# A hybrid decoder block on one core: four weight stages stream 512 columns per matmul instead of 256

## The chip, the core and the metric

The kernel runs on one core of a Trainium2 chip. Time is device microseconds of one launch; the median of three runs is given. The engines of the core work side by side: PE (TensorE) multiplies, DVE (VectorE) and ACT (ScalarE) do elementwise work and read the matmul results from the eight PSUM banks (128 partitions x 512 float32 each), POOL (GpSimd) does a little, SP (SyncE) issues the transfers from memory. They are tied together by semaphores that the kernel sets by hand.

## The reference, cut to what matters

One decoder layer on 256 tokens of width 2048, in float32:

```python
y = rmsnorm(x); u = y @ w_in                   # queries, keys, values, gates of three branches
mk, mv = split(rmsnorm(mem) @ w_mem_kv)        # memory keys and MEMORY VALUES, 1024 columns each
a = sparse_attention(...)                      # 8 heads
r = group_norm(retention(q, k, v)) * silu(g)   # g: RETENTION GATE, 1024 columns of u
m = memory_attention(mq, mk, mv)               # 4 heads
s = sum(sigmoid(gate_b) * (branch_b @ w_br_b)) # merged, 256 x 2048
x = x + rmsnorm(s @ w_o)                       # OUTPUT PROJECTION, 2048 x 2048
z = rmsnorm(x) @ w_up                          # 2048 x 11264
z = gelu(conv3(z[:, :5632])) * conv3(z[:, 5632:])
out = x + rmsnorm(z @ w_down)                  # DOWN PROJECTION, 5632 x 2048
```

The four products in capitals are those that the change touches.

## The kernel before, in words

**Three products for one.** Each float32 operand is split into a rounded part (`_hi`) and the remainder (`_lo`), both in the type fp32r. A product is then hi x hi + hi x lo + lo x hi: three matmuls in a row, each with a weight load of its own (PEld in the profile).

**Quads and chunks.** The weights come in quads: 4 chunks of 512 KB, each 4 row tiles (of 128) x 256 columns. Chunk c has slot c of `wraw`, `whi` and `wlo`. For a chunk, SP loads `wraw[c]` (line 255 or 265), ACT makes `whi[c]` (line 461), DVE makes `wlo[c]` (line 679), and PE runs 24 matmuls of 256 columns: 4 row tiles x 2 halves x 3 products. ACT's step for the next quad's chunk c waits until PE has finished chunk c of this quad (`pe_done`), DVE's step waits for ACT's, SP's next load waits for DVE's (`lo_done`). The helper `ahead(q, chunks)` stands for this work on the next quad, and what else ACT and DVE do is written between such calls.

**Two forms.** In `chunk_t` (lines 1064 to 1066) a 128 x 128 piece of the weights is the stationary operand and the 256 tokens stream. In `chunk_n` (lines 1077 to 1079) 128 tokens are stationary and 256 weight columns stream. The four stages of the change use `chunk_n`. Each result of a quad fills one bank: 256 columns for tokens 0 to 127, then 256 for tokens 128 to 255.

**The four stages.** Memory values (`mv`, 4 quads), retention gate (`rg`, 4 quads) and output projection (`wo`, 8 quads) accumulate a quad in bank 0 or 1, in turn. A bank is drained while the next quad runs in the other: `mv` by one DVE copy (line 690), `rg` by ACT's tanh (line 570) and DVE's product (line 866), `wo` by two ACT squares (line 613) and a DVE product (line 953). PE waits for `evac[b]` before it takes bank b again. The down projection runs in 11 steps of 2 quads. Here each chunk is a group of 256 output columns over 512 rows of `w_down`, goes to bank 2 + g % 4, and is added to `M` by DVE (line 1015); `s_dn` counts these adds, and group g waits for the add of group g - 4.

**Loops.** Between two down steps stand 4 quads of the up projection (`chunk_t`). Two steps (1152 matmuls) form the body of one hardware loop of 5 trips at the end of the kernel; the 11th down step follows it. `mv`, `rg` and most of `wo` are hardware loops of 2, 2 and 3 trips with 192 matmuls in a body. After `wo` and after the last down step there is a mean square (DVE lines 703 and 704, POOL line 386) and a normalisation (line 970) before PE or the output can go on. After `rg` the first thing in the retention is `inner` (line 1314), two matmuls into bank 3 behind the first chunk of the next quad.

Of the kernel before, what the change touches and what calls it, by code (L numbers as in the profile page):

```python
# [25 lines left out]
P = 128  # L26
# [32 lines left out]
PHASES = [("mq", 4, 4), ("mk", 4, 4), ("mv", 4, 4), ("nq", 4, 4), ("kv0", 3, 3), ("mix", 7, 3),  # L59
          ("rqk", 4, 4), ("rv", 4, 4), ("rg", 4, 4),  # L60
          ("bg0", 8, 8), ("br0", 4, 8), ("bg1", 8, 8), ("br1", 4, 8), ("bg2", 8, 8), ("br2", 4, 8),
          ("wo", 8, 8), ("up0", 4, 4), ("ffn", 6 * (STEPS - 1), 4 * (STEPS - 1)), ("dn", 2, 0)]
# [63 lines left out]
def build(nc, x, mem, w_in, cmp_pe_k, cmp_w1_k, cmp_w2_k, cmp_pe_v, cmp_w1_v, cmp_w2_v, rel_bias,  # L126
# [3 lines left out]
    with ctx:  # L130
# [71 lines left out]
        s_swap, s_rgt, s_stats = sem("halves_swapped"), sem("ret_gate_tanh"), sem("stats_made")  # L202
# [45 lines left out]
        def _(sp):  # L248
            def quad(q, src):

                for c in range(4):
                    if q:

                        sp.wait_ge(lo_done, 4 * (q - 1) + c + 1)
                    sp.dma_start(wraw[:, c], src(c)).then_inc(loaded[c], 16)  # L255

            def loop(q0, trips, per, sources):

                with sp.Fori(0, trips) as i:
                    free = [sp.snap(4 * per * i + (4 * (q0 - 1) + k + 1)) for k in range(4 * per)]  # L260
                    src = sources(i)
                    for j in range(per):
                        for c in range(4):
                            sp.wait_ge(lo_done, free[4 * j + c])
                            sp.dma_start(wraw[:, c], src[j](c)).then_inc(loaded[c], 16)

            def cols(w, base, count=2):
# [4 lines left out]
                return sources  # L272

# [32 lines left out]
            loop(Q0["mk"], 4, 2, cols(w_mem_kv[:, :, :], 0))  # L306
# [16 lines left out]
            loop(Q0["rg"], 2, 2, cols(w_in, C_RQ + 8 * GW))  # L323
# [15 lines left out]
            for n in range(2):  # L339
                quad(Q0["wo"] + n, lambda c: rows(w_o, 4 * c, GW * n))  # L340
# [3 lines left out]
            loop(Q0["wo"] + 2, 3, 2, cols(w_o, 2 * GW))  # L344
# [18 lines left out]
            loop(Q0["ffn"], STEPS - 1, 6, step)  # L363
            for j in range(2):
                quad(Q0["dn"] + j, down((STEPS - 1) * 512)[j])
# [89 lines left out]
        def _(act):  # L455
# [107 lines left out]
            with act.Fori(0, 2) as i:  # L563
                for j in range(2):
                    q = 2 * i + (Q0["rg"] + j)
# [41 lines left out]
            with act.Fori(0, 4) as i:  # L607
                for j in range(2):
                    q = 2 * i + (Q0["wo"] + j)
                    ahead(q, (0, 1, 2))  # L610
                    act.wait_ge(pe_done, 4 * q + 4)
# [4 lines left out]
                    ahead(q, (3,))  # L616
# [38 lines left out]
            ahead(Q0["dn"], (0,))  # L655
            for g in range(8):
                if g < 3:
                    ahead(Q0["dn"], (g + 1,))
                act.wait_ge(s_dn, 4 + 8 * (STEPS - 1) + g + 1)
                for t in range(TT):  # L660
                    e = nc.scalar.activation(h_hi[:, 2 * g + t, :], M[:, t, GW * g:GW * (g + 1)], ACT.Square,
# [766 lines left out]
```

## Time and profile before

| | |
|---|---|
| median of 3 runs | 1865.62 us (1865.15 to 1865.78) |
| profiled execution: span, first to last instruction | 1862.0 us |
| what lies around it (median less span) | 3.6 us |
| PE busy | 1775.8 us, 95% (14,505 matmuls) |
| DVE busy | 1057.9 us, 57% |
| ACT busy | 789.5 us, 42% |
| DMA | 328.19 MB, 57.6% of the engines' time |

The whole duration of the profiled execution is not listed apart from its span; the 3.6 us are the median less the span. A matmul's row shows its start and its length; because matmuls are pipelined, the distance between the starts of two of them is what one costs, and the length is longer than that. The granted clock of TensorE is 1.0 at 2.4 GHz and 0.5 at 1.2 GHz.

### The profile page before, as it was taken

Reading aid. Unit: us, or ns where it says so; the run is one execution under the profiler, and the core shown is the slowest. Engines: PE = TensorE matmul, PEld = TensorE weight load, DVE = VectorE, ACT = ScalarE, POOL = GpSimd, SP = SyncE. Lnnn points to the kernel's source line nnn. Section 1 sums busy time; section 2 is a strip of 40 time slices with the busy share of each in tenths; the row PEclk is TensorE's granted clock in tenths of the full one; section 3 lists DMA queues with packets and bytes.
Section 4 is the critical chain, followed back from the end, with each engine's and each line's share of the span. In section 5 each row is a group of like instructions: output and inputs, shape, how many; then the busy total and the mean of one; then the engine's idle time right before and its main releaser. Section 6 shows DMA issues by size and latency. Waiting matters only on the chain.

```text
span 1862.0 us, 36931 instructions
## 1 busy us (share of the span) xinstructions
PE 1775.8 (95%) x14505; PEld 1763.1 (95%) x14505; DVE 1057.9 (57%) x1321; ACT 789.5 (42%) x1036; POOL 42.2 (2%) x47
## 2 busy tenths in 40 slices
PE   7599999999999999999999799989999998999997
PEld 6499999899999999999999799989989998998997
DVE  5254557566565444454564566655665664664666
ACT  5233335444433334434444454434444443443443
POOL 0000100000031000000000000000000000000000
PEclk9799999999999999999999899999999999999999
DMA  8655457645555566666575356655555554555553
GB/s 244 140 183 184 138 158 242 188 136 153 174 163 164 184 181 180 196 192 183 174 233 186 124 182 196 188 160 172 184 185 158 184 183 154 182 185 161 181 182 113
DMA packets 321460, 328.19 MB, mean 176 GB/s; under 512 B 12239, under 2 KB 318528, under 8 KB 320832
## 3 DMA queue, kind: packets, MB, share of 16 engines
q1 hardware_dynamic: 321344, 326.45, 57.6%
q8 instruction: 96, 1.57, 0.3%
q14 instruction: 20, 0.16, 0.0%
HBM read 321.69 MB, written 3.67 MB: 175 GB/s over the span
## 4 chain that ended last, share of the span: by engine, by line
PE 51%; issue 42%; DVE 2%; DMA 2%; SPq 1%; ACT 1%; POOL 0%; DVEq 0%; POOLq 0%; ACTq 0%
PE bank L1064 11%; PE bank L1066 11%; PE bank L1065 11%; PE bank L1077 5%; PE bank L1079 5%; PE bank L1078 5%; DMA wraw<-in_w_in 1%; SPq L255 1%; DVE wlo L679 1%; DVE arena L970 0%; ACT whi L461 0%; PE bank L1131 0%; PE bank L1193 0%; PE bank L1295 0%; PE bank L1274 0%
## 5 line engine op out<-in xcount | busy, mean ns | idle before, releaser
L679 DVE TENSOR_TENSOR wlo<-wraw,whi 128x1024 fp32r<-128x1024 f32 x592 | 728.7, 1236 | 655.1 <-ACT whi L461 653.5
L461 ACT ACTIVATE whi<-wraw 128x1024 fp32r<-128x1024 f32 x592 | 625.3, 1059 | 946.7 <-PE bank L1066 649.4
L1064 PE MATMUL bank<-h_hi,whi 128*128 128x256 f32 x2688 | 769.0, 286 | 10.4 <-DVE wlo L679 7.5
L1065 PE MATMUL bank<-h_lo,whi 128*128 128x256 f32 x2688 | 764.6, 284 | 9.6 <-issue 9.6
L1066 PE MATMUL bank<-h_hi,wlo 128*128 128x256 f32 x2688 | 764.5, 284 | 0.0
L1064 PEld LDWEIGHTS bank<-h_hi,whi 128*128 128x128 f32 x2688 | 520.0, 193 | 12.8 <-DVE wlo L679 8.1
L1066 PEld LDWEIGHTS bank<-h_hi,wlo 128*128 128x128 f32 x2688 | 520.0, 193 | 10.0 <-issue 10.0
L1065 PEld LDWEIGHTS bank<-h_lo,whi 128*128 128x128 f32 x2688 | 519.8, 193 | 0.2
L1077 PE MATMUL bank<-whi,r_hi 128*128 128x256 f32 x704 | 199.2, 283 | 0.0
L1078 PE MATMUL bank<-wlo,r_hi 128*128 128x256 f32 x704 | 199.2, 283 | 0.0
L1079 PE MATMUL bank<-whi,r_lo 128*128 128x256 f32 x704 | 199.2, 283 | 0.0
L1077 PEld LDWEIGHTS bank<-whi,r_hi 128*128 128x128 f32 x704 | 135.2, 192 | 0.0
L1078 PEld LDWEIGHTS bank<-wlo,r_hi 128*128 128x128 f32 x704 | 135.2, 192 | 0.0
L1079 PEld LDWEIGHTS bank<-whi,r_lo 128*128 128x128 f32 x704 | 135.2, 192 | 0.0
L1064 PE MATMUL bank<-m_hi,whi 128*128 128x256 f32 x384 | 108.7, 283 | 0.0
L1065 PE MATMUL bank<-m_lo,whi 128*128 128x256 f32 x384 | 108.7, 283 | 0.0
L1066 PE MATMUL bank<-m_hi,wlo 128*128 128x256 f32 x384 | 108.7, 283 | 0.0
L1077 PE MATMUL bank<-whi,m_hi 128*128 128x256 f32 x384 | 108.7, 283 | 0.0
L1078 PE MATMUL bank<-wlo,m_hi 128*128 128x256 f32 x384 | 108.7, 283 | 0.0
L1079 PE MATMUL bank<-whi,m_lo 128*128 128x256 f32 x384 | 108.7, 283 | 0.0
L1077 PE MATMUL bank<-whi,h_hi 128*128 128x256 f32 x320 | 92.4, 289 | 1.1 <-DVE wlo L679 1.1
L1079 PE MATMUL bank<-whi,h_lo 128*128 128x256 f32 x320 | 91.0, 285 | 0.0
(202 smaller groups left out, 1759.2 us busy)
## 6 DMA issues: line engine op xcount, KB each, us to landing
wraw<-in_w_in SPq DMA_DIRECT2D x200, 512.0 KB, 3.7
wraw<-in_w_up SPq DMA_DIRECT2D x176, 512.0 KB, 3.8
wraw<-in_w_down SPq DMA_DIRECT2D x88, 512.0 KB, 3.4
wraw<-in_w_mem_kv SPq DMA_DIRECT2D x32, 512.0 KB, 4.6
wraw<-in_w_o SPq DMA_DIRECT2D x32, 512.0 KB, 3.5
wraw<-in_w_br_mem SPq DMA_DIRECT2D x16, 512.0 KB, 3.4
wraw<-in_w_br_nsa SPq DMA_DIRECT2D x16, 512.0 KB, 4.0
wraw<-in_w_br_ret SPq DMA_DIRECT2D x16, 512.0 KB, 3.3
```

Source lines behind the costliest of these rows:

```text
L255: sp.dma_start(wraw[:, c], src(c)).then_inc(loaded[c], 16)
L461: nc.scalar.activation(whi[:, c], wraw[:, c], ACT.Copy).then_inc(hi_done, 1)
L679: V.tensor_tensor(wlo[:, c], wraw[:, c], whi[:, c].bitcast(F32), ALU.subtract).then_inc(lo_done, 1)
L1064: T.matmul(o, wh, xh, start=first and k == 0 and t == 0, stop=False, skip_group_check=True)
L1065: T.matmul(o, wh, xl, start=False, stop=False, skip_group_check=True)
L1066: e = T.matmul(o, wl, xh, start=False, stop=last and k == CK - 1, skip_group_check=True)
L1077: T.matmul(o, xh, wh, start=first and k == 0 and t == 0, stop=False, skip_group_check=True)
L1078: T.matmul(o, xh, wl, start=False, stop=False, skip_group_check=True)
L1079: e = T.matmul(o, xl, wh, start=False, stop=last and k == CK - 1, skip_group_check=True)
```

## The change

The four stages stream 512 weight columns per matmul. A chunk is still 512 KB, but now 2 row tiles x 512 columns, and has 12 matmuls (2 token halves x 2 row tiles x 3 products). A result of 512 columns fills two banks, one for each half of the tokens. Two quads together (`octet`, 8 chunks) make one 512-column group in banks 0 and 1 or 2 and 3. In the down projection a group of 512 columns has two chunks and the bank pair 2, 3 or 4, 5; group n waits for the adds of group n - 2. The drains become two instructions for each pair. The loops of `mv`, `rg` and `wo` are written out.

```diff
@@ phases: (name, quads, groups that are drained)
-... ("mv", 4, 4) ... ("rg", 4, 4) ... ("wo", 8, 8)
+... ("mv", 4, 2) ... ("rg", 4, 2) ... ("wo", 8, 4)
@@ slot views and loads
+        def wide(buf, c):
+            return buf[:, c].rearrange("p k n -> p (k n)").rearrange("p (k n) -> p k n", k=2)
+            def wide_cols(w, base):
+                def sources(i):
+                    at = sp.snap(2 * GW * i + base)
+                    return [lambda c, j=j: rows(w, 8 * j + 2 * c, at, 2 * GW, 2) for j in range(2)]
+                return sources
-            loop(Q0["mk"], 4, 2, cols(w_mem_kv[:, :, :], 0))
+            loop(Q0["mk"], 2, 2, cols(w_mem_kv[:, :, :], 0))
+            loop(Q0["mv"], 2, 2, wide_cols(w_mem_kv[:, :, :], MH * MD), into_wide)
...
-                return [lambda c, j=j: w[:, :, (4 * j + c) * GW:(4 * j + c + 1) * GW] for j in range(2)]
+                return [lambda c, j=j: w[:, 2 * (c % 2):2 * (c % 2) + 2, (4 * j + 2 * (c // 2)) * GW:(4 * j + 2 * (c // 2) + 2) * GW]
+                        for j in range(2)]
@@ ACT: retention gate and output projection
-                    ahead(q, (0, 1, 2))
-                    act.wait_ge(pe_done, 4 * q + 4)
-                    act.wait_ge(evac[1 - j], i + (G0["rg"] // 2 + j))
-                    nc.scalar.activation(work[:, W_RGT:W_RGT + 512], ps[j][:, :], ACT.Tanh, scale=0.5).then_inc(s_rgt, 1)
-                    ahead(q, (3,))
+                ahead(q)
+                ahead(q + 1, (0, 1, 2))
+                act.wait_ge(pe_done, 4 * (q + 1) + 4)
+                for t in range(TT):
+                    if 2 * i + t:
+                        act.wait_ge(s_rgv, 2 * i + t)
+                    nc.scalar.activation(work[:, W_RGT:W_RGT + 512], ps[2 * i + t][:, :], ACT.Tanh, scale=0.5).then_inc(s_rgt, 1)
+                ahead(q + 1, (3,))
...
-                    for t in range(TT):
-                        e = nc.scalar.activation(work[:, 512 * j + S * t:512 * j + S * (t + 1)], bank(j, t), ACT.Square,
-                                                 accum_out=sq[:, 0, t, bass.ds(2 * i + j, 1)])
-                    e.then_inc(s_sq, 1)
+                for t in range(TT):
+                    nc.scalar.activation(work[:, 512 * t:512 * (t + 1)], ps[2 * (i % 2) + t][:, :], ACT.Square,
+                                         accum_out=sq[:, 0, t, i:i + 1]).then_inc(s_sq, 1)
@@ DVE: memory values
+            for i in range(2):
+                q = Q0["mv"] + 2 * i
+                ahead(q)
+                ahead(q + 1, (0, 1, 2))
+                dve.wait_ge(pe_done, 4 * (q + 1) + 4)
+                ch.add(V.tensor_copy(by_head(A_MV + 1024 * i, 0), ps[2 * i][:, :].rearrange("p (h n) -> p h n", h=2)))
+                ch.link(V.tensor_copy(by_head(A_MV + 1024 * i, 1), ps[2 * i + 1][:, :].rearrange("p (h n) -> p h n", h=2)))
+                dve.sem_inc(evac[i], 1)
+                ahead(q + 1, (3,))
@@ DVE: down projection, one step (see the order below)
-            def down_group(q, g):
-                dve.wait_ge(pe_done, 4 * q + (g + 1))
-                f = M[:, :, GW * g:GW * (g + 1)]
-                return V.tensor_tensor(f, bank(2 + g % 4), f, ALU.add)
+            def down_group(q, g, t):
+                dve.wait_ge(pe_done, 4 * q + (2 * g + 2))
+                f = M[:, t, 512 * g:512 * (g + 1)]
+                return V.tensor_tensor(f, ps[2 + 2 * (g % 2) + t][:, :], f, ALU.add)
@@ PE
+            def chunk_w(q, c, b, hi_, lo_, k0, first, last):
+                pe.wait_ge(lo_done, 4 * q + (c + 1))
+                vh, vl = wide(whi, c), wide(wlo, c)
+                for t in range(TT):
+                    o = ps[b + t][:, :]
+                    for k in range(2):
+                        xh, xl = hi_(k0 + k)[:, t * P:(t + 1) * P], lo_(k0 + k)[:, t * P:(t + 1) * P]
+                        T.matmul(o, xh, vh[:, k, :], start=first and k == 0, stop=False)
+                        T.matmul(o, xh, vl[:, k, :], start=False, stop=False)
+                        e = T.matmul(o, xl, vh[:, k, :], start=False, stop=last and k == 1)
+                e.then_inc(pe_done, 1)
+            def octet(q, b, before, x_, fresh=False, tiles_ready=None):
+                for n in range(2):
+                    if fresh or n == b:
+                        pe.wait_ge(evac[n], before)
+                for c in range(8):
+                    if tiles_ready is not None:
+                        pe.wait_ge(tiles_ready[0], tiles_ready[1] + c + 1)
+                    chunk_w(q + c // 4, c % 4, 2 * b, *x_, 2 * c, c == 0, c == 7)
-            quads(chunk_n, "mv", 2, MM)
+            for i in range(2):
+                octet(Q0["mv"] + 2 * i, i, G0["mv"] // 2, MM, i == 0)
...
                     def inner():
                         pe.wait_ge(r_q, r + 1)
+                        pe.wait_ge(evac[1], G0["bg0"] // 2)
...
-                for g in range(8):
-                    pe.wait_ge(s_dn, 8 * s + g + 1)
-                    chunk_n(q + g // 4, g % 4, 2 + g % 4, *YR, 4 * u, True, True)
+                for n in range(4):
+                    pe.wait_ge(s_dn, 8 * s + (2 * n + 2))
+                    for k in range(2):
+                        chunk_w(q + n // 2, 2 * (n % 2) + k, 2 + 2 * (n % 2), *YR, 4 * u + 2 * k, k == 0, k == 1)
```

On PE, in the last down step, a bank was kept for 24 matmuls of 256 columns. These are the rows before where bank 2 gives way to bank 3 (lines 1077 to 1079 are the three products of `chunk_n`):

```order
L1077 MATMUL bank2<-whi,r_hi 128x256
L1078 MATMUL bank2<-wlo,r_hi 128x256
L1079 MATMUL bank2<-whi,r_lo 128x256
L1077 MATMUL bank3<-whi,r_hi 128x256
L1078 MATMUL bank3<-wlo,r_hi 128x256
L1079 MATMUL bank3<-whi,r_lo 128x256
```

And of the change, at the same place (lines 1124 to 1126 are the three products of `chunk_w`):

```order
L1124 MATMUL bank2<-whi,r_hi 128x512
L1125 MATMUL bank2<-wlo,r_hi 128x512
L1126 MATMUL bank2<-whi,r_lo 128x512
L1124 MATMUL bank3<-whi,r_hi 128x512
L1125 MATMUL bank3<-wlo,r_hi 128x512
L1126 MATMUL bank3<-whi,r_lo 128x512
```

Each bank now has 6 matmuls of 512 columns and gives way to the other of its pair, and comes back once more for the second chunk of the group.

On DVE, the start of the last down step before, with the step on the next weights (line 679), the add (line 1015) and the product with the gain (line 1038):

```order
L1020 COMPARE_AND_BRANCH
L679 TENSOR_TENSOR wlo<-wraw,whi 128x1024
L1015 TENSOR_TENSOR arena<-bank2,arena 128x2x256
L679 TENSOR_TENSOR wlo<-wraw,whi 128x1024
L1015 TENSOR_TENSOR arena<-bank3,arena 128x2x256
L1038 TENSOR_TENSOR arena<-arena,tables 128x2x256
```

The same place of the change (696 is the step on the weights, 1046 the add, 1070 the product):

```order
L1051 COMPARE_AND_BRANCH
L696 TENSOR_TENSOR wlo<-wraw,whi 128x1024 x2
L1046 TENSOR_TENSOR arena<-bank2,arena 128x512
L1046 TENSOR_TENSOR arena<-bank3,arena 128x512
L696 TENSOR_TENSOR wlo<-wraw,whi 128x1024 x2
L1046 TENSOR_TENSOR arena<-bank4,arena 128x512
L1046 TENSOR_TENSOR arena<-bank5,arena 128x512
L1070 TENSOR_TENSOR arena<-arena,tables 128x512 x2
```

The number of steps and adds is the same, but they come in pairs: two steps on the weights, then the two adds of a group.

## Rows read from the trace of the kernel before

**Rows 1.** The page, busy time by engine.

```profile
PE 1775.8 (95%) x14505; PEld 1763.1 (95%) x14505; DVE 1057.9 (57%) x1321; ACT 789.5 (42%) x1036; POOL 42.2 (2%) x47
```

**Rows 2.** Windows: length, busy us (count) by engine (PE first), clock, DMA share.

```profile
146.00:169.00 23.00, 23.00 (x194) 23.00 (x194) 11.19 (x10) 8.47 (x8) 0.00 (x0) 1.00 0.57 184
...
1247.00:1393.00 146.00, 141.05 (x1152) 140.76 (x1152) 85.87 (x103) 62.09 (x70) 0.00 (x0) 0.98 0.56 174
```

**Rows 3.** Timeline (start, length), memory values at full clock.

```profile
168.97 0.28 PE L1078 MATMUL bank<-wlo,m_hi 128*128 128x256 f32 x1
...
169.09 0.28 PE L1079 MATMUL bank<-whi,m_lo 128*128 128x256 f32 x1
```

**Rows 4.** Timeline, up projection at half clock.

```profile
1251.30 0.41 PE L1064 MATMUL bank<-h_hi,whi 128*128 128x256 f32 x1
...
1251.51 0.41 PE L1065 MATMUL bank<-h_lo,whi 128*128 128x256 f32 x1
```

**Rows 5.** Groups of instructions, float32 matmuls: busy us, mean ns, then idle before.

```profile
L1211 PE MATMUL bank<-work 128*128 128x256 f32 x32 | 7.6, 379 | 0.0
...
L1276 PE MATMUL bank<-kc,work 128*128 128x15 f32 x16 | 3.0, 262 | 0.0
```

**Rows 6.** Timeline, float32 matmuls of memory attention and of compressed keys.

```profile
207.27 1.89 PE L1211 MATMUL bank<-work 128*128 128x256 f32 x8
...
464.03 0.37 PE L1276 MATMUL bank<-kc,work 128*128 128x15 f32 x2
```

**Rows 7.** Timeline, all engines, from the memory values to the queries.

```profile
192.13 0.28 PE L1079 MATMUL bank<-whi,m_lo 128*128 128x256 f32 x1
...
192.56 0.69 DVE L690 COPY arena<-bank 128x512 f32 x1 [0.67 <-PE bank L1079]
...
193.51 0.48 PE L1193 MATMUL bank<-arena,work 128*128 x1 [1.10 <-DVE arena L690]
```

**Rows 8.** Timeline, ACT and DVE at the end of the retention gate.

```profile
525.21 0.60 ACT L570 ACTIVATE work<-bank 128x512 f32<-128x512 f32 x1 [1.90 <-PE bank L1079]
...
525.95 0.69 DVE L866 SCALAR_TENSOR_TENSOR arena<-work,bank 128x512 f32 x1 [1.38 <-ACT work L570]
```

**Rows 9.** Timeline, DVE where the output projection starts.

```profile
951.55 0.69 DVE L929 SCALAR_TENSOR_TENSOR work<-arena,bank 128x512 f32<-128x512 f32 x1 [1.27 <-PE bank L1066]
```

**Rows 10.** Timeline, ACT and DVE at the end of the output projection.

```profile
1043.67 0.38 ACT L613 ACTIVATE work<-bank 128x256 f32<-128x256 f32 x1 [1.91 <-PE bank L1079]
...
1045.14 0.16 DVE L703 TENSOR_REDUCE st<-sq 128x2 f32<-128x16 f32 x1
```

**Rows 11.** Timeline, ACT and DVE in a down step.

```profile
1301.03 0.63 ACT L637 ACTIVATE work<-work 128x512 f32<-128x512 f32 x1
...
1305.96 1.23 DVE L679 TENSOR_TENSOR wlo<-wraw,whi 128x1024 fp32r<-128x1024 f32 x1 [0.21 <-ACT whi L461]
...
1307.10 0.68 DVE L1015 TENSOR_TENSOR arena<-bank,arena 128x512 f32<-128x512 f32 x1
```

**Rows 12.** Timeline, PE at the second and the fifth trip of the last loop.

```profile
1247.60 0.38 PE L1064 MATMUL bank<-h_hi,whi 128*128 128x256 f32 x1 [2.29 <-issue]
...
1250.91 0.37 PE L1065 MATMUL bank<-h_lo,whi 128*128 128x256 f32 x1 [2.58 <-issue]
...
1684.20 0.38 PE L1064 MATMUL bank<-h_hi,whi 128*128 128x256 f32 x1 [2.43 <-DVE wlo L679]
```

**Rows 13.** Who waited for whom, PE: us in total, times, longest.

```profile
PE bank L1065 <- issue: 9.6, 4, 2.6
```

**Rows 14.** The page, queue that loads instructions: packets, MB, share.

```profile
q8 instruction: 96, 1.57, 0.3%
```

**Rows 15.** Timeline, DVE at the end of the kernel.

```profile
1849.30 0.69 DVE L1015 TENSOR_TENSOR arena<-bank,arena 128x512 f32<-128x512 f32 x1 [1.59 <-PE bank L1079]
...
1850.97 0.17 DVE L703 TENSOR_REDUCE st<-sq 128x2 f32<-128x16 f32 x1 [0.38 <-ACT h_hi L661]
...
1852.52 0.75 DVE L970 SCALAR_TENSOR_TENSOR arena<-arena,st 128x512 f32<-128x512 f32 x1 [0.58 <-POOL st L386]
```

More of the change, by code:

```diff
@@ L248, in _, with quad @@
         def _(sp):
-            def quad(q, src):
+            def quad(q, src, dst=lambda c: wraw[:, c]):
                 for c in range(4):
@@ L254, in quad, with loop @@
                         sp.wait_ge(lo_done, 4 * (q - 1) + c + 1)
-                    sp.dma_start(wraw[:, c], src(c)).then_inc(loaded[c], 16)
-            def loop(q0, trips, per, sources):
+                    sp.dma_start(dst(c), src(c)).then_inc(loaded[c], 16)
+            def loop(q0, trips, per, sources, dst=lambda j, c: wraw[:, c]):
                 with sp.Fori(0, trips) as i:
@@ L338, in _ @@
                 loop(Q0[f"br{n}"], 2, 2, pairs)
-            for n in range(2):
-                quad(Q0["wo"] + n, lambda c: rows(w_o, 4 * c, GW * n))
+            for j in range(2):
+                quad(Q0["wo"] + j, lambda c: rows(w_o, 8 * j + 2 * c, 0, 2 * GW, 2), lambda c: wide(wraw, c))
             sp.wait_ge(s_mgl, KT // 2)
             quarters(X, x, s_x)
-            loop(Q0["wo"] + 2, 3, 2, cols(w_o, 2 * GW))
+            loop(Q0["wo"] + 2, 3, 2, wide_cols(w_o, 2 * GW), into_wide)
             def up_col(n):
@@ L362, in step @@
                 return [lambda c, o=o: rows(w_up, 4 * c, o) for o in at] + down(sp.snap(512 * i))
-            loop(Q0["ffn"], STEPS - 1, 6, step)
+            loop(Q0["ffn"], STEPS - 1, 6, step, step_dst)
             for j in range(2):
-                quad(Q0["dn"] + j, down((STEPS - 1) * 512)[j])
+                quad(Q0["dn"] + j, down((STEPS - 1) * 512)[j], lambda c: wide(wraw, c))
             for n, (t, at, width) in enumerate(OUT_PARTS):
@@ L946, in _ @@
             dve.wait_ge(s_gpost, 16)
-            def wo_group(i, j):
-                q = 2 * i + (Q0["wo"] + j)
-                ahead(q, (0, 1, 2))
-                dve.wait_ge(s_sq, 2 * i + (j + 1))
-                V.tensor_tensor(M[:, :, bass.ds(512 * i + GW * j, GW)], bank(j),
-                                GP[:, bass.ds(512 * i + GW * j, GW)].unsqueeze(1).to_broadcast([P, TT, GW]), ALU.mult).then_inc(evac[j], 1)
-                return q
-            with dve.Fori(0, 3) as i:
-                for j in range(2):
-                    ahead(wo_group(i, j), (3,))
-            ahead(wo_group(3, 0), (3,))
-            last = wo_group(3, 1)
-            mean_square(2, 8, (s_sq, 8))
+            for i in range(4):
+                q = Q0["wo"] + 2 * i
+                ahead(q)
+                ahead(q + 1, (0, 1, 2))
+                for t in range(TT):
+                    dve.wait_ge(s_sq, 2 * i + t + 1)
+                    ch.add(V.tensor_tensor(M[:, t, 512 * i:512 * (i + 1)], ps[2 * (i % 2) + t][:, :], GP[:, 512 * i:512 * (i + 1)], ALU.mult))
+                ch.wait()
+                dve.sem_inc(evac[i % 2], 1)
+                if i < 3:
+                    ahead(q + 1, (3,))
+            mean_square(2, 4, (s_sq, 8))
             dve.wait_ge(evac[0], G0["up0"] // 2)
@@ L974, in _ @@
                 post(X, k % 2, 1024 * (k // 2), 1024, s_x2)
-            ahead(last, (3,))
+            ahead(Q0["wo"] + 7, (3,))
             mean_square(3, 2, (s_ssq, 12))
@@ L1178, in _ @@
             quads(chunk_t, "mk", 2, MM)
-            quads(chunk_n, "mv", 2, MM)
+            for i in range(2):
+                octet(Q0["mv"] + 2 * i, i, G0["mv"] // 2, MM, i == 0)
             with pe.Fori(0, 2) as i:
@@ L1303, in _ @@
                         quad((chunk_t, chunk_n)[g], q, j, i + G0[ph] // 2, H, {-1: scores, NSA_BEFORE[-1]: transposes, 3: output})
-            quads(chunk_n, "rg", 2, H)
+            for i in range(2):
+                octet(Q0["rg"] + 2 * i, i, G0["rg"] // 2, H, i == 0)
             with pe.Fori(0, 2) as i:
@@ L1345, in _ @@
                             chunk_t(2 * i + (Q0[f"br{n}"] + j), c, c // 2, *y, 4 * (c % 2), c % 2 == 0, c % 2 == 1)
-            quad(chunk_n, Q0["wo"], 0, G0["wo"] // 2, MM, tiles_ready=(s_mgl, 0))
-            quad(chunk_n, Q0["wo"] + 1, 1, G0["wo"] // 2, MM)
-            quads(chunk_n, "wo", 3, MM, 2)
+            for i in range(4):
+                octet(Q0["wo"] + 2 * i, i % 2, G0["wo"] // 2 + i // 2, MM, i == 0, (s_mgl, 0) if i == 0 else None)
             def up_quads(q, s):
```

100 lines of the change are left out of this document (54 added, 46 removed).

## The prediction

> **What bounds the kernel now.** I read the busy times first, then windows by stage, then the timeline of PE inside a stage, then the waits of PE. PE is busy 95% of the span [rows 1]. In the memory values it works 23.00 of 23 us at clock 1.0, DVE 11.19, ACT 8.47 [rows 2]: two quads of 96 matmuls in 23.04 us, nothing but PE. One matmul of 256 columns starts 0.120 us after the one before [rows 3]. The same holds through the four stages. So the first question is what the 0.120 is made of, and the second where PE is made to wait.
>
> At half clock the distance is 0.213 [rows 4], which is 256 columns at 1.2 GHz and nothing over. At full clock the columns would take 0.107; 0.013 more is there. If those 0.013 were a cost on top of the columns, half clock would show at least 0.226. It does not, so beside the columns runs something that needs about 0.120 by itself and is hidden at half clock. The weight load is the candidate: each matmul has one. The float32 matmuls speak for it: two records of 15 columns take 0.37 with one 0.262 long, so 0.11 apart with hardly a column [rows 5, 6]; and of the long kind eight take 1.89 with one 0.379 long, so 1.51 / 7 = 0.216 apart [rows 5, 6], 518 cycles of 2.4 GHz, with a weight load each time that costs nothing visible. A float32 matmul appears twice in the records, so I take these as 512 cycles of streaming each.
>
> **Part 1, the matmuls.** The stages have 4 + 4 + 8 + 22 = 38 quads of 96 matmuls, 3648. They become 1824 of 512 columns. The trace has no fp32r matmul of 512 columns. Bounds: 0.2133 (columns alone at 2.4 GHz) and 0.240 (twice the 0.120, if the rate per column were the limit). Nearest rows: 0.216, a 512-cycle matmul with its own load. I take 0.216. Old 3648 x 0.120 = 437.8, new 1824 x 0.216 = 394.0: 43.8 us less. Bounds of the term: 48.7 and 0.
>
> The Trainium skill (TensorE: Matmul & The Clock Gate, section Back-to-back issue gap) gives a gap of N / 2.4 + 2.5 ns. By that rule two matmuls of 256 cost 218.3 ns and one of 512 costs 215.8, so the change would save 2.5 ns per pair, 4.6 us in all; an estimate from the page. The trace agrees at 512 cycles (216) and not at 256, where it has 120 instead of 109, so the measured distance decides. The same section names 131 ns for N=512 in a real kernel; nothing in this trace comes near that, [rows 6] has 216.
>
> **Part 2, new waits of PE.** A group now fills two banks, so where a stage begins or ends PE meets a drain that the other bank used to hide.
> - Keys to values: the first octet needs banks 0 and 1, and the last key quad has just ended in bank 1. What this costs is shown where values turn to queries: the last matmul starts at 192.13, the copy at 192.56 (0.69 long), PE again at 193.51 [rows 7], 1.38 instead of 0.12. So +1.26.
> - Values to queries: this wait is there already, with one copy; now two. A second copy adds what DVE needs per instruction, 0.6 to 0.69: +0.6.
> - Gate to retention: tanh starts at 525.21, some 0.3 after PE is through (a drain in [rows 7] starts as late), and takes 0.60; the product starts at 525.95 and takes 0.69 [rows 8]. There are now two of each in a chain, since both use one buffer: about 2 x 1.7 = 3.5 to the release. `inner` stands behind one chunk of 24 x 0.120 = 2.88. +0.7. Behind it PE holds the rest of the quad; ACT's step for that quad's fourth chunk comes 1.7 later but is due 8.6 after the stage's end, so it costs nothing.
> - Branches to output projection: the first octet needs bank 1 from the last branch group. That drain (951.55, 0.69 long [rows 9]) is of the same kind as above: +1.3. Its chunks wait for two merged tiles each, which come long before.
> - End of the output projection: PE is idle here in any case, and the chain is squares, product, sum [rows 10]. Before: two squares of 256 from 1043.67, sum at 1045.14. Now two of 512 (0.63 for one of that width [rows 11], and its read of the sum 0.2) and one product after the second: +0.8.
> - End of the kernel: DVE's last add at 1849.30, sum at 1850.97 [rows 15]. Now two adds of 0.68, then two products with the gain for the group before (0.6 each) stand in front of the sum: it moves to about +2.75 from +1.97 after PE's end; two products of the last group stand behind it where POOL's power (done 1.55 after the sum [rows 15]) hides one: +0.9.
> Together 1.26 + 0.6 + 0.7 + 1.3 + 0.8 + 0.9 = 5.6 us. Bounds 3 and 9.
>
> Inside the down steps nothing is late, by my sum. Group n + 2 needs the adds of group n. After PE ends group n, ACT's step is done at 1.3, DVE's (1.23, the add follows it after 1.14) at 2.6, two adds of 0.68 at 3.9 [rows 11], seen by PE at about 4.05. PE meanwhile runs group n + 1, 24 x 0.216 = 5.18. 1.1 us in hand, and the convolution before (DVE busy until about 5 after the up quad's end) ends before the first group does. The loads: 512 KB per 2.59 instead of 2.88 us takes the DMA share from 0.57 [rows 2] to 0.63, in lines of 2 KB instead of 1. Octets have a slack of 8 chunks. Cost zero; if that cover went, each wait would be paid 22 times.
>
> **Part 3, the loop.** The last loop has a pause that the others have not. At each of the four jumps PE rests twice: before the first matmul (2.29, 2.43) and after the fourth (2.58) [rows 12]; the second kind sums to 9.6 us in four [rows 13], put down to no semaphore. Three trips of 1152 matmuls lie between 1247.60 and 1684.20 [rows 12]: 436.60 against 3 x 138.24 = 414.72, so a jump costs 7.3 us, of which some 4.9 is rest and the remainder half clock after it (clock 0.98 over a trip [rows 2], matmuls 0.213 apart [rows 4]). The body has 2374 PE instructions; the loops of 395 to 481 show no such pause. The instruction queue moved 96 packets of 16 KB [rows 14]. I read it so: a long body is loaded anew at each jump in pieces, the first rest is for the piece with the loop's head, the second for the next piece. Then the second rest begins where the head's piece ends. In the changed program the head stands 26 instructions earlier, while the start of the program is unchanged. If the pieces lie where they lay, 13 more matmuls come before the second rest: 13 x 0.120 = 1.56 of its 2.4 is covered. Half clock after shorter rests I take at half, 0.9 less. 2.45 x 4 = 9.8 us less. Bounds: 0 (nothing moves) and 14 (no half clock left).
>
> [...]
>
> **Sum.** The profiled span is 1862.0, and 3.6 lie between it and the median of 1865.62. In the span: 1862.0 - 43.8 + 5.6 - 9.8 = 1814.0; with 3.6, 1817.6. I say 1818.
>
> **Rivals.**
> - A cost on top: the new matmul takes 0.2267 (0.2133 + 0.0133). For: the 0.013 exists at full clock. Against: half clock has none of it. Gain 1824 x 0.0133 = 24.3, time 1865.6 - 24.3 + 5.6 - 9.8 = 1837. Chance 0.07.
> - A limit per column: fp32r takes 0.469 ns per column however many, 0.240 in all. For: no faster column is in the trace at this type; half clock would hide it too. Against: 15-column matmuls are 0.11 apart without columns. Time 1865.6 + 5.6 - 9.8 = 1861. Chance 0.04.
> - The loop's pauses vanish, since the shorter body stays loaded: 4 x 7 = 28 less instead of 9.8. For: bodies up to 481 do not pause, and the trace has none between that and 2374. Against: 1982 is nearer to the long one. Time 1865.6 - 43.8 + 5.6 - 28 = 1799. Chance 0.07. [...]
> - The loop's pauses stay as they are: 1827. Chance 0.08.
> - Slower: the adds of a group reach PE late in each down step, because two steps on the weights now stand before them on DVE. For: only two groups are in rotation instead of four. It needs 48 us over 22 waits, 2.2 each, so adds 3.3 later than I reckon; at 2.4 each 1818 + 53 = 1871. Against: 1.1 in hand and DVE 59% busy there (85.87 of 146 [rows 2]). Chance 0.02.
> - My forecast, 0.72, with a range of its own of 1811 to 1826.
>
> The range for 8 in 10: 1808 to 1832; it takes in the unmoved pauses and leaves out the vanished ones and the two limits of the matmul. About 0.2% (3.7 us) is what a measurement can tell from no change. Faster 0.96, same 0.02, slower 0.02.
>
> **What would show it.** Matmuls of 512 columns 0.216 apart in the memory values: right; 0.227 or 0.240: a rival. An idle of 1.3 at the first value matmul, at the first output matmul, and about 0.7 before `inner`. No wait of PE for the adds within down steps. In the last loop, four rests of 2.4 before the first matmul and shorter ones behind the seventeenth, where the fourth had them. It is wrong if PE idles between down groups, if the rests stand elsewhere, or if a drain that I called hidden appears in PE's waits.

## The result and the profile after

The changed kernel takes 1835.21 us, median of 4 runs (1834.54 to 1836.62), against 1865.38 of before on the same chip (1863.12 to 1865.78): ratio 0.9841, interval 0.9827 to 0.9855, 30.2 us less. The forecast was 1818, 47.6 less than the 1865.62 it started from, and 1835 lies outside its range of 1808 to 1832. The page of the changed kernel, busy time by engine (answers to [rows 1]), and its instruction queue (answers to [rows 14]):

```profile
PE 1750.0 (95%) x12681; PEld 1663.7 (91%) x12681; DVE 1057.7 (58%) x1321; ACT 786.8 (43%) x1004; POOL 40.7 (2%) x47
...
q8 instruction: 86, 1.41, 0.3%
```

1824 matmuls fewer, yet PE is as busy as before by share. The windows of the memory values and of the second trip of the last loop, with the columns of [rows 2]:

```profile
146.00:169.00 23.00, 22.06 (x102) 18.29 (x101) 10.39 (x10) 8.48 (x8) 0.00 (x0) 1.00 0.57 178
1240.00:1379.00 139.00, 136.34 (x961) 128.28 (x961) 85.78 (x102) 61.80 (x71) 0.00 (x0) 1.00 0.60 182
```

PE still fills its stretch but for the rests. What a matmul costs is read from three neighbours in the timeline (start, length), the place of [rows 3]:

```profile
175.01 0.39 PE L1126 MATMUL bank<-whi,m_lo 128*128 128x512 f32 x1
...
175.24 0.39 PE L1124 MATMUL bank<-whi,m_hi 128*128 128x512 f32 x1
...
175.47 0.39 PE L1125 MATMUL bank<-wlo,m_hi 128*128 128x512 f32 x1
```

0.23 apart, not 0.216. From 147.95 to 191.33 there are 191 distances: 43.38 / 191 = 0.2271. e1 below has the distance with less noise, 0.2267. So two matmuls of 256 (0.240) became one of 0.2267, and a pair is worth 13.3 ns. The whole of Part 1 is 1824 x 0.0133 = 24.3 us.

The two stage starts that now wait for a drain, in the timeline of all engines; the last key quad, the values, the queries, and then the last branch group and the output projection (answers to [rows 7, 9]):

```profile
146.73 0.28 PE L1100 MATMUL bank<-m_hi,wlo 128*128 128x256 f32 x1
147.95 0.47 PE L1124 MATMUL bank<-whi,m_hi 128*128 128x512 f32 x1 [0.94 <-issue]
...
191.33 0.39 PE L1126 MATMUL bank<-whi,m_lo 128*128 128x512 f32 x1
...
191.76 0.69 DVE L780 COPY arena<-bank 128x512 f32<-128x512 f32 x1 [0.40 <-PE bank L1126]
...
192.36 0.68 DVE L781 COPY arena<-bank 128x512 f32<-128x512 f32 x1
...
193.37 0.48 PE L1252 MATMUL bank<-arena,work 128*128 x1 [1.65 <-DVEq L782]
...
949.76 0.28 PE L1100 MATMUL bank<-r_hi,wlo 128*128 128x256 f32 x1
...
950.20 0.69 DVE L962 SCALAR_TENSOR_TENSOR work<-arena,bank 128x512 f32<-128x512 f32 x1 [1.27 <-PE bank L1100]
951.05 0.47 PE L1124 MATMUL bank<-whi,m_hi 128*128 128x512 f32 x1 [1.01 <-issue]
```

From start to start: 1.22 in place of 0.12, 2.04 in place of 1.38, 1.29 in place of 0.12. Behind the gate the drains are a chain through one buffer (answers to [rows 8]), and the first trip of the retention loop takes 29.54 in place of 29.10, 0.44 more. Only 0.20 of it stands at `inner` itself, where the forecast looked for 0.7 (from the matmul before to `inner` 0.32 in place of 0.12):

```profile
523.36 0.60 ACT L591 ACTIVATE work<-bank 128x512 f32<-128x512 f32 x1 [1.60 <-PE bank L1126]
523.99 0.69 DVE L896 SCALAR_TENSOR_TENSOR arena<-work,bank 128x512 f32<-128x512 f32 x1 [0.97 <-ACT work L591]
524.71 0.60 ACT L591 ACTIVATE work<-bank 128x512 f32<-128x512 f32 x1 [0.76 <-DVE arena L896]
```

The end of the kernel (answers to [rows 15]):

```profile
1819.84 0.39 PE L1126 MATMUL bank<-whi,r_lo 128*128 128x512 f32 x1
...
1820.27 1.29 DVE L1046 TENSOR_TENSOR arena<-bank,arena 128x512 f32<-128x512 f32 x2 [2.95 <-PE bank L1126]
...
1821.47 1.28 DVE L1070 TENSOR_TENSOR arena<-arena,tables 128x512 f32<-128x512 f32 x2
...
1822.67 0.15 DVE L724 TENSOR_REDUCE st<-sq 128x2 f32<-128x8 f32 x1
```

Two adds, two products, then the sum of squares (L724), 2.83 after the last matmul's start in place of 1.99, so 0.84 later; 1833.7 - 1819.84 = 13.9 to the end of the span, in place of 13.0. Who waits for whom on PE (answers to [rows 13]):

```profile
PE bank L1099 <- issue: 7.9, 4, 2.2
PE bank L1098 <- issue: 4.1, 5, 1.2
...
PE bank L1124 <- issue: 1.9, 2, 1.0
PE bank L1252 <- DVEq L782: 1.6, 1, 1.6
```

L1124 opens a group of 512 columns, in the down steps too; its two waits are the two stage starts above, so no down group waits for its adds. The first two rows are the rests of the last loop (one wait of 0.2 in the second row stands elsewhere). At its first jump (answers to [rows 12]):

```profile
1238.48 0.39 PE L1126 MATMUL bank<-whi,r_lo 128*128 128x512 f32 x1
1240.07 0.38 PE L1098 MATMUL bank<-h_hi,whi 128*128 128x256 f32 x1 [1.20 <-issue]
...
1241.96 0.28 PE L1098 MATMUL bank<-h_hi,whi 128*128 128x256 f32 x1
1244.14 0.39 PE L1099 MATMUL bank<-h_lo,whi 128*128 128x256 f32 x1 [1.90 <-issue]
```

Sixteen matmuls, 1.89 us, now lie between the rests, where four lay. The five trips take 695.3 (1102.98 to 1798.31) against 678.4 of matmuls: 16.9 over, where before had 719.1 against 691.2: 27.9 over. The loop gives back 11.0.

By the profile the sum is -24.3 for the matmuls, +4.9 for the edges (1.10 + 0.66 + 0.44 + 1.17 + 0.71 at the end of the output projection + 0.84), -11.0 for the loop, +0.9 in the stretch of the key and value mix and +0.7 before the first matmul, both outside the change: -28.8; the spans differ by 28.3. The medians differ by 30.2. Every run listed with its span takes 1.9 to 2.0 us longer than that span, so the profiled execution of before, with a span of 1862.0, took about 1864 (an estimate) and was a quick one: its span is 3.6 under the median, the new one's 1.5.

### The profile page after: what moved, and what is told of

It is laid out like the page before. It is cut to its first block, busy times and chain, and to the rows that moved or that the text cites. A ratio compares the mean times of both kernels' runs of the same rounds, so it can differ in the third digit from the quotient of the medians.

```text
span 1833.7 us, 32977 instructions
## 1 busy us (share of the span) xinstructions
PE 1750.0 (95%) x12681; PEld 1663.7 (91%) x12681; DVE 1057.7 (58%) x1321; ACT 786.8 (43%) x1004; POOL 40.7 (2%) x47
## 4 chain that ended last, share of the span: by engine, by line
PE 93%; DVE 2%; DMA 2%; issue 1%; SPq 1%; ACT 1%; POOL 0%; DVEq 0%; ACTq 0%; POOLq 0%
PE bank L1098 21%; PE bank L1099 21%; PE bank L1100 21%; PE bank L1124 8%; PE bank L1125 8%; PE bank L1126 8%; DMA wraw<-in_w_in 1%; PE bank L1111 1%; PE bank L1112 1%; PE bank L1113 1%; SPq L259 1%; DVE arena L1001 0%; PE bank L1189 0%; ACT whi L481 0%; DVE wlo L696 0%
## 5 line engine op out<-in xcount | busy, mean ns | idle before, releaser
L1124 PE MATMUL bank<-whi,r_hi 128*128 128x512 f32 x352 | 137.1, 389 | 0.0
L1125 PE MATMUL bank<-wlo,r_hi 128*128 128x512 f32 x352 | 137.1, 389 | 0.0
L1126 PE MATMUL bank<-whi,r_lo 128*128 128x512 f32 x352 | 136.9, 389 | 0.0
L1021 DVE SCALAR_TENSOR_TENSOR work<-bank,conv,work 128x254 f32<-128x254 f32 (+1 forms) x176 | 76.5, 476 | 5.8
L1126 PEld LDWEIGHTS bank<-whi,r_lo 128*128 128x128 f32 x352 | 66.1, 188 | 13.9
L1124 PEld LDWEIGHTS bank<-whi,r_hi 128*128 128x128 f32 x352 | 66.1, 188 | 13.4
L1125 PEld LDWEIGHTS bank<-wlo,r_hi 128*128 128x128 f32 x352 | 66.1, 188 | 13.3
L1124 PE MATMUL bank<-whi,m_hi 128*128 128x512 f32 x192 | 74.8, 390 | 1.9 <-issue 1.9
L1125 PE MATMUL bank<-wlo,m_hi 128*128 128x512 f32 x192 | 74.7, 389 | 0.0
L1126 PE MATMUL bank<-whi,m_lo 128*128 128x512 f32 x192 | 74.7, 389 | 0.0
L1098 PEld LDWEIGHTS bank<-m_hi,whi 128*128 128x128 f32 x384 | 73.7, 192 | 0.0
```

The costliest lines, as they stand in the source:

```text
L1021: e = V.scalar_tensor_tensor(y, bank(j, t)[:, 0:S - d], conv[:, tap, bass.ds(4 * s + (44 * j + 2 * a + t), 1)], y, ALU.mult, ALU.add)
L1098: T.matmul(o, wh, xh, start=first and k == 0 and t == 0, stop=False, skip_group_check=True)
L1124: T.matmul(o, xh, vh[:, k, :], start=first and k == 0, stop=False)
L1125: T.matmul(o, xh, vl[:, k, :], start=False, stop=False)
L1126: e = T.matmul(o, xl, vh[:, k, :], start=False, stop=last and k == 1)
```

## The experiments

**e1_probe: what a matmul costs.** The theory after the result: a cost on top of the columns. Bursts of 32 matmuls stand at the end of the changed kernel; their results are not used.

```
+ burst(32, lambda k: T.matmul(ps[6][:, :], wt(k), W5[k], start=True, stop=True))
+ burst(32, lambda k: T.matmul(ps[6][:, 0:384], wt(k), W5[k][:, 0:384], ...))
+ ... 256, 128 and 64 columns; 64 weight columns; two banks in turn; one weight tile; float32
```

> The changed kernel with bursts of matmuls behind the last down step, whose results nobody reads; its time says nothing, the distance between starts in each burst does. In the changed kernel a 512-column fp32r matmul costs 226.7 ns, not the 216 of my forecast, so 13.3 ns stand on top of the columns at full clock. Theory A, a fixed cost per fp32r matmul that half clock does not show: 512 columns 227, 384 columns 173, 256 columns 120, the same with 64 weight columns instead of 128, the same with one stationary tile for all, the same with two banks in turn; float32 data 216; at half clock 427 and 213. Theory B, the cost is the last part of a 128-column weight load that the stream cannot hide: with 64 weight columns the distance falls to about 220 and 113. Theory C, the cost is the write into the bank that the matmul before is still writing: with banks 6 and 7 in turn it falls to 216. For 128 and 64 columns all three expect a floor near 112, which the 15-column matmuls showed.

The timeline of PE; x32 is a burst (the float32 ones are 16 matmuls, two records each):

```profile
1819.17 7.42 PE L1446 MATMUL bank<-whi,m_hi 128*128 128x512 f32 x32
1826.42 5.73 PE L1447 MATMUL bank<-whi,m_hi 128*128 128x384 f32 x32
1832.00 3.99 PE L1448 MATMUL bank<-whi,m_hi 128*128 128x256 f32 x32
1835.82 3.69 PE L1449 MATMUL bank<-whi,m_hi 128*128 128x128 f32 x32
...
1851.86 3.80 PE L1452 MATMUL bank<-whi,m_hi 128*64 128x256 f32 x32
...
1870.03 7.07 PE L1455 MATMUL bank<-whi,m_hi 128*128 128x256 f32 x32
1876.93 13.90 PE L1456 MATMUL bank<-whi,m_hi 128*128 128x512 f32 x32
```

From start to start of neighbours: 0.227 at 512 columns, 0.173 at 384, 0.120 at 256, each 13.3 ns over the columns at 2.4 GHz; 0.111 at 128 and at 64, a floor. Two banks in turn and one weight tile again and again: 0.227 as well. Float32: 0.216 and 0.429, 2.5 over. So at full clock, with 128 weight columns, an fp32r matmul costs 13.3 ns over its columns whatever their number from 256 up, and float32, from which the forecast took its 0.216, doesn't pay it: theory A, and not C. With 64 weight columns neither A nor B fits: 256 columns take 0.114 (L1452), as B said, but 512 take 0.230 on average outside the stretch at half clock, where B said 0.220 and A 0.227. The burst of 512 with 64 weight columns ran for a while at clock 0.50, that is 1.2 GHz; the same stretch in windows of two lengths:

```profile
1843.38 2.11 PE L1451 MATMUL bank<-whi,m_hi 128*64 128x512 f32 x5
```

```profile
1843.38 1.26 PE L1451 MATMUL bank<-whi,m_hi 128*64 128x512 f32 x3
```

Two distances more are 0.85, 0.427 each: 512 / 1.2 and nothing over, as [rows 4] had it at 256 with 128 weight columns.

**e8_probe_types: is it the type, or the weight load?**

```
+ burst(32, lambda k: T.matmul(ps[6][:, :], wb(k), WB[k], ...))             # bf16, also 256, 128
+ burst(32, lambda k: T.matmul(ps[6][0:32, :], wt(k, 32), W5[k], ...))      # 96, 32 weight columns
+ burst(32, lambda k: T.matmul(ps[6][:, :], wt(k)[0:64], W5[k][0:64], ...)) # 64 rows
```

> The changed kernel with bursts of 32 matmuls at its end (their results are not used; the time is longer by them). Distances at full clock. If the 13.3 ns are a matter of the type: bf16 takes 213 + 2.5 at 512 columns and 107 + 2.5 at 256; if of any matmul with a weight load of 128 columns: 227 and 120 in bf16 too. With 96 and 32 weight columns or 64 rows in fp32r: 227 and 120 if the 13.3 do not depend on the load, 216 and 109 if they are a part of it. The last two bursts repeat 256 and 512 columns with 128 weight columns: 120 and 227.

```profile
1818.67 7.08 PE L1452 MATMUL bank<-whi,m_hi 128*128 128x512 bf16 x32
1825.59 3.66 PE L1453 MATMUL bank<-whi,m_hi 128*128 128x256 bf16 x32
...
1864.54 4.09 PE L1461 MATMUL bank<-whi,m_hi 128*128 128x256 f32 x32
1868.47 7.44 PE L1462 MATMUL bank<-whi,m_hi 128*128 128x512 f32 x32
```

Bf16 takes 0.216 at 512 columns, 0.109 at 256 and 0.056 at 128; fp32r takes 0.120 and 0.227 in the same program. So the cost goes with the type. The bf16 bursts don't have the same weight loads, though: a load of 128 columns (PEld) is 97 to 98 ns long in bf16 and 188 to 192 in fp32r. Two things speak against the load as the cause: float32 in e1 has loads of 190 ns and pays 2.5 only, and shorter loads of fp32r (161 ns with 96 weight columns, 108 with 32) bring neither 0.216 nor 0.109, but 0.230 and 0.116 with 96, 0.232 and 0.118 with 32 (unsteady distances). Yet 256 columns do get cheaper with each of them, most with 64 (0.114), so a part of the load isn't excluded there. With 64 rows it stays 0.227 and 0.120. What in fp32r costs the 13.3 isn't shown.

**e2_before_unrolled and e3_after_unrolled: what the loop costs in each kernel.** The last loop is written out on PE alone, so PE never jumps in it; one condition inside the body is adapted to that.

```
- with pe.Fori(0, (STEPS - 1) // 2) as i:
+ for i in range((STEPS - 1) // 2):
```

> The kernel before with the last loop written out on PE alone (the other engines keep their loops), so that PE never jumps back in it. Theory L, the rests and the half clock after them come from loading the body anew at each jump: all of the 27.9 us over 5 x 138.24 go, time about 1838 (ratio 0.985), no rest of over 1 us of PE between 1100 and 1800. Rival, the rests belong to the other engines' jumps (ACT's and DVE's loops end at the same place): at least the first rest of each trip stays, 4 x 2.4 = 10 us of the 28, time about 1848 or more.

> The changed kernel with the last loop written out on PE alone. Five trips take 695.3 us there against 5 x 135.7 = 678.4 for the matmuls, so theory L expects 16.9 us less: 1835.2 - 16.9 = 1818. The rival (rests of the other engines' jumps) expects the first rests of 1.0 to 1.5 to stay: about 1824.

Before written out takes 1835.32 (ratio 0.9842, 0.9826 to 0.9858), the changed kernel written out 1815.75 (0.9736, 0.972 to 0.9753). Windows of the second trip's place, PE alone, of the changed kernel written out:

```profile
1240.00:1379.00 139.00, 139.00 (x989) 1.00 0.61 187
```

No rest, clock 1.00, and the same for the kernel before: theory L holds in both, and the rival with the other engines' jumps (1848, 1824) is out. That PE's instructions are loaded anew at the jumps shows in the queue that loads instructions (packets, MB, share; answers to [rows 14]), first of the kernel before written out, then of the changed kernel written out:

```profile
q8 instruction: 84, 1.38, 0.3%
```

```profile
q8 instruction: 76, 1.25, 0.3%
```

A body that stayed loaded would need fewer packets than one written out five times. It needs more: 96 against 84 in before, 86 against 76 in the changed kernel, and from 1247 to 1393 us, before's second trip, 12 against 9. The loop cost 30 us in before (29.3 against the 1864.63 of before on e2's chip) and 19.5 in the changed kernel. Without the loop the change is worth 1835.32 - 1815.75 = 19.6, and 24.3 - 4.9 = 19.4: the first two parts add up with no loop in them. And one line on one engine gives as much as the whole change.

**e5_down_alone and e6_three_alone: which part of the change shortens the rests.** Theory S says where the loop's head stands on PE, theory Q how long body and matmuls are. The first has the wide matmuls in the down steps only, the second everywhere else only.

```
# e5, against the kernel before (PE's part)
- for g in range(8):
-     pe.wait_ge(s_dn, 8 * s + g + 1)
-     chunk_n(q + g // 4, g % 4, 2 + g % 4, *YR, 4 * u, True, True)
+ for n in range(4):
+     pe.wait_ge(s_dn, 8 * s + (2 * n + 2))
+     for k in range(2):
+         chunk_w(q + n // 2, 2 * (n % 2) + k, 2 + 2 * (n % 2), *YR, 4 * u + 2 * k, k == 0, k == 1)
# e6, against the changed kernel: the same lines the other way round
...
```

> Only the down projection streams 512 columns (with its drains of 512 and the tail at the kernel's end); memory values, gate and output projection stay as before. Both theories: 1056 matmuls of 512 columns in place of 2112 of 256 save 1056 x 13.3 ns = 14.0 us, the kernel's end costs 0.95. They differ in the last loop. Its body is as long as in the changed kernel (1022 PE instructions in place of 1222), but its head stands where it stood before. Theory Q (what shortens the rests is what is queued at the jump: matmuls twice as long): first rests 1.1 to 1.6 us in place of 2.6 to 2.9, the loop gives back about 11 us as in the changed kernel, time 1865.4 - 14.0 + 0.95 - 11 = 1841. Theory S (where the head stands decides: 12 or 13 more matmuls ahead of the second rest): first rests shorter as well, but the second stands behind the 4th matmul and the half clock follows all four; 5 us back, time 1847.

> Memory values, retention gate and output projection stream 512 columns, the down projection stays at 256. Both theories: 768 matmuls of 512 columns save 768 x 13.3 ns = 10.2 us; the drains at the edges of these stages cost 1.1 + 0.66 + 0.44 + 1.17 + 0.71 = 4.1 (as read in the changed kernel), net -6.1. In the last loop the head moves on PE as in the changed kernel, the body is the old one. Theory Q: the loop costs what it cost, time 1865.4 - 6.1 = 1859. Theory S: second rests behind the 16th matmul, half clock half as often, 5 to 6 us less: 1854.

e5 takes 1851.92 (0.993, 0.9913 to 0.9946), where S said 1847 and Q 1841; e6 takes 1846.38 (0.9903, 0.9886 to 0.992), where S said 1854 and Q 1859. More than half of the matmuls' gain is in the down steps, yet e6, which has them as before, is the faster of the two. The first jump of the kernel with wide down steps alone, PE's timeline:

```profile
1243.71 0.39 PE L1115 MATMUL bank<-whi,r_lo 128*128 128x512 f32 x1
1245.24 0.38 PE L1087 MATMUL bank<-h_hi,whi 128*128 128x256 f32 x1 [1.14 <-issue]
...
1245.70 0.28 PE L1087 MATMUL bank<-h_hi,whi 128*128 128x256 f32 x1
1249.04 0.37 PE L1088 MATMUL bank<-h_lo,whi 128*128 128x256 f32 x1 [3.06 <-issue]
```

The first rest is short, as in the changed kernel, but the second took what the first gave: 5.33 from the last matmul to the resume, 5.88 in before (1245.03 to 1250.91), 5.65 in the changed kernel (1238.48 to 1244.14). In the kernel with three wide stages the head is moved and the matmuls of the down steps are short:

```profile
1239.72 0.28 PE L1108 MATMUL bank<-whi,r_lo 128*128 128x256 f32 x1
1242.22 0.38 PE L1093 MATMUL bank<-h_hi,whi 128*128 128x256 f32 x1 [2.23 <-issue]
...
1245.39 0.41 PE L1093 MATMUL bank<-h_hi,whi 128*128 128x256 f32 x1
1245.94 0.39 PE L1094 MATMUL bank<-h_lo,whi 128*128 128x256 f32 x1
```

6.22 in all, and nearly all of the sixteen matmuls in it ran at half clock (0.213 apart), so that hardly a second rest is left. Over their matmuls the five trips take 28.4 us with wide down steps alone (706.8 - 678.4) and 16.5 with three wide stages (707.7 - 691.2), where before has 27.9: the first kernel is -14.0 + 0.8 with a loop that gives nothing, the second -10.2 + 4.1 with a loop that gives 11.5. So Q falls, and of S the main claim holds, that the place of the head decides. Both of its numbers were off by more than the runs scatter, 5 and 5 to 6 us for the loop, because they counted the shorter first rest as a gain of its own and the moved head for too little. The form of S that follows, about 5.6 us from the last matmul to the second resume, was made after these two runs; the next two test it.

**e4_head_at_edge, e9_head_back_26, e10_head_back_12: the head alone moved.** Increments of an unused semaphore on PE ahead of the changed kernel's last loop, 40, 26 and 12 of them.

```
+ for _ in range(40):
+     pe.sem_inc(s_fill, 1)
  with pe.Fori(0, (STEPS - 1) // 2) as i:
```

> The changed kernel with 40 semaphore increments on PE ahead of the last loop, so that the loop's head stands 4 instructions behind an edge of the 256-instruction pieces and the body of 1982 touches 8 pieces instead of 9. Theory F1 (the pieces are loaded anew whenever a body is longer than what is held, and 8 pieces are held with room for none ahead): the first rest of each trip stays, the second moves from behind the 16th matmul to behind about the 124th and is mostly hidden there by instructions already queued, so some 4 x 2 = 8 us less: 1827. Theory F2 (8 pieces fit): no rest at all, no new load in the loop, 16.9 less: 1818. Rival F3 (the second rest does not depend on the edge): 1835.

> The changed kernel with 26 semaphore increments on PE ahead of the last loop, which puts the loop's head where it stood before the change. Theory S (from the last matmul of a trip to the end of the second rest it is about 5.6 us whatever PE does in between, so a jump costs 5.6 less the matmuls between the rests, plus the half clock): second rest behind the 4th matmul, 0.45 us of work between the rests in place of 1.89, half clock for 2.5 to 5.7 us after all four. The loop loses 7.3 us per jump in place of 4.2, time 1835.2 + 12 = 1847. Theory Q (length of body or of the queued matmuls): 1835.4.

> The same with 12 increments: the head stands half way. Theory S: second rest behind the 10th matmul, 1.17 us of work between the rests, 0.7 more of rest per jump and some more half clock: 1835.2 + 2.9 + 3 = 1841. Theory Q: 1835.3.

In this order the times are 1829.28 (0.9808, 0.9792 to 0.9825), 1849.38 (0.9918, 0.9901 to 0.9934) and 1841.45 (0.9873, 0.9857 to 0.989). For 40 increments F1 said 1827, and F2 (1818) and F3 (1835) are out; the instruction queue agrees, with 82 packets the body was still loaded anew. For 26 and 12, S said 1847 and 1841, Q 1835. With 26 the second rest stands one matmul earlier than in before, behind the third; PE's timeline:

```profile
1240.99 0.38 PE L1098 MATMUL bank<-h_hi,whi 128*128 128x256 f32 x1 [1.06 <-issue]
1245.06 0.58 PE L1098 MATMUL bank<-h_hi,whi 128*128 128x256 f32 x1 [3.46 <-issue]
```

By jump, from the traces (matmuls between the rests; range of last matmul to resume over the four jumps; mean loss of trips two to four against their matmuls):

| kernel | between | last to resume, us | loss per trip, us |
|---|---|---|---|
| before | 4 | 5.6 to 6.0 | 7.3 |
| e5, down alone | 4 | 5.3 to 5.7 | 7.3 |
| e9, 26 increments | 3 | 5.3 to 5.7 | 7.1 |
| e10, 12 increments | 10 | 5.0 to 5.7 | 5.7 |
| the change | 16 | 5.1 to 5.7 | 4.4 |
| e6, three alone | 16 | 5.6 to 6.2 (three jumps) | 4.2 |
| e4, 40 increments | no second rest | 1.3 to 1.6 | 1.4 |

Between before and the change lie 2.9 us per trip. Twelve more matmuls are 1.4 of them; about 0.9 is half clock, and some 0.4 is the time from the last matmul to the resume, which is a little shorter where wide matmuls end the trip (5.9 on average in before, 5.5 in the change). Half clock followed every jump with 3 to 10 matmuls between the rests (2.3 to 5.8 us of matmuls 0.213 apart) and two of four in the changed kernel. The increments also have a price where the loop begins, which no expectation had. With 40, PE rests once for 4.57 us there, with 14 matmuls at half clock behind it; 12 us fewer in the jumps leave 5.9 net. With 26 it rests for 2.30 there (1101.66 to 1103.96), which is most of what 1849.38 has over the 1847; with 12 or none there is no such rest. Why, isn't shown.

**e7_best: the drains moved behind other banks.** The changed kernel with the loop written out, and the first wide group of values and of the output projection in banks 2 and 3.

```
- octet(Q0["mv"] + 2 * i, i, G0["mv"] // 2, MM, i == 0)
+ octet(Q0["mv"] + 2 * i, 1 - i, [(0, G0["mv"] // 2), (1, G0["mv"] // 2)] if i else [], MM)
```

> The changed kernel with the last loop written out on PE, and the first wide group of the memory values and of the output projection in banks 2 and 3 in place of 0 and 1, the second in 0 and 1, and so on. PE then starts these stages while the last narrow group drains. If the new idle times at the two stage starts (1.10 and 1.17 us) are those drains, they go, and some 0.4 of the 0.66 at values to queries too, since only bank 0 of the first query group waits: 1815.75 - 2.7 = 1813. Rival: the wait moves to the second wide group's banks or to the weights, then 1815.5.

It takes 1811.54 (1811.51 to 1812.39; ratio 0.9716, 0.97 to 0.9732), 4.2 less than e3 and 1.5 less than the 1813 expected. The rows L1124 and L1252 of PE's waits are gone. Where values turn to queries, the last matmul of the values starts at 189.99, and the first of the queries opens this row of PE's timeline:

```profile
190.22 1.89 PE L1250 MATMUL bank<-arena,work 128*128 x8
```

0.23 from start to start, where the changed kernel has 2.04 and before 1.38: not 0.4 went here but 1.8, the wait of before with it, and 1.10 + 1.17 + 1.8 = 4.1 is what was measured. This kernel beats both others, by 53.8 and 23.7 us.

## Why the prediction was wrong

- **Part 1, the step that failed.** "I take 0.216" was the price of a float32 matmul. fp32r costs 0.2267, and the term is 24.3 in place of 43.8: 19.5 us, more than the whole miss of 17.2 (1835.2 against 1818). e1 shows it at three lengths in one burst each. The argument against the right rival was that half clock shows none of the 13 ns. That reading is true (0.213 and 0.427), but it doesn't exclude a fixed cost that stands at full clock alone. The matmul of the same type was in the rows at one length only; with one length any split between columns and fixed cost fits, and the forecast filled the gap from another type. The rival was priced at 1837, 1.8 from the result, with a chance of 0.07; with nothing of the type at a second length it should have had a third at least, and the range should have reached it. Its own bounds (48.7 and 0) held the value.
- The rule in the Trainium skill (TensorE: Matmul & The Clock Gate, section Back-to-back issue gap), N / 2.4 + 2.5 ns, which the page gives for the isolated matmul, fits bf16 (216, 109) and float32 counted by its cycles (216 for 512, 429 for 1024) to the nanosecond; fp32r measures N / 2.4 + 13.3. The measurement decides for this kernel. The 131 ns for N=512 stands in none of these runs.
- **Part 2 was right**: 5.6 forecast, 4.9 read. Term by term 1.26 / 1.10, 0.6 / 0.66, 0.7 / 0.44, 1.3 / 1.17, 0.8 / 0.71, 0.9 / 0.84. At `inner` itself only 0.20 of the 0.44 stands, where 0.7 was looked for. At the kernel's end the sum of squares came 2.83 after the last matmul's start, where the forecast had 2.75. e7 shows by taking them away that the waits at the two stage starts were drains, and that the one at values to queries was too.
- **The down steps** have no wait for the adds, as forecast, and the rival on the slower side is out.
- **Part 3 was right in its mechanism and near in size**, 9.8 forecast and 11.0 read, but not in how the rests divide. e2 and e3 show that the rests come from PE's jumps, the packets of the instruction queue that the body is loaded anew, e9 and e10 that the shifted head is what brings the gain. The second rest stands behind the 16th matmul, where the shift of 26 instructions was to bring it behind the 17th. The half clock gave about 0.9 per jump, as taken. But the forecast left the first rests at 2.4 and cut the second to some 0.8. In PE's waits the four first rests fell from 9.8 to 3.9 us and the four second ones only from 9.6 to 7.9. Together that is 1.9 per jump in place of the 1.56 forecast; that a wrong split gave so near a sum is in part luck. What the forecast had not seen: the two rests aren't two prices; the time from the last matmul to the second resume stays near 5.6, and a shorter first rest only makes the second longer.
- A small second error: 3.6 was added between span and median; the new kernel has 1.5. That is 2.1 towards a lower time.

Together: +19.5 (matmul) - 0.7 (edges) - 1.2 (loop) - 2.1 (span to median) + 1.6 (outside the change) = 17.1, of 17.6 (1835.2 - 1817.6, the forecast's sum before it was rounded to 1818). The other 0.5 isn't placed.

What stays open: which part of fp32r costs 13.3 ns at full clock and none at half, its columns' stream or its weight load; why two of the changed kernel's jumps are followed by half clock and two not; why PE rests where the loop begins with 26 and 40 increments and not with 12.

## What to carry to other kernels

Price a matmul from one of the same type; where the trace has that type at one length only, columns and fixed cost can't be told apart, and both must stay in the range with real weight. Per pair merged the gain is the fixed cost alone, 13.3 ns here. Each stage start that must now wait for the last group's drain costs about 1.1 us, what some 80 merged pairs give, and e7 shows that another order of banks can take it away. Before tuning a long loop's body, look for PE rests put down to "issue" behind its jumps: writing a loop out on that one engine was worth as much here as four rewritten stages.

## What was not expected of the hardware

- A fixed 13.3 ns on each fp32r matmul with 128 weight columns at full clock (0.120 at 256 columns, 0.173 at 384, 0.227 at 512), 2.5 in bf16 and float32; a floor of 0.111 at 64 and 128 fp32r columns, where bf16 has 0.056 at 128.
- At a jump of a body of 1982 or 2374 instructions PE's stream came back for good 5.0 to 6.2 us after the last matmul wherever there was a second rest, with 3, 4, 10 or 16 matmuls between the rests; what lies between the two rests is free.
- Fewer weight columns made fp32r of 512 columns slower (0.230 to 0.232 in place of 0.227), and of 256 columns faster (0.114 with 64, 0.116 with 96, 0.118 with 32, in place of 0.120).
- 40 semaphore increments that nothing waits for, ahead of a loop, took 5.9 us off the kernel; 26 of them added 14.2.
